# Hybrid attention layer on one core: the bank of weighted values is emptied by ScalarE, and GpSimd adds its pieces

## What is computed

```
...
def stick_breaking_attention(q, k, v):
...
        log_beta = jax.nn.log_sigmoid(z)
        log_stay = jnp.where(mask, jax.nn.log_sigmoid(-z), 0.0)
        later = lax.cumsum(log_stay, axis=3, reverse=True) - log_stay
        weights = jnp.where(mask, jnp.exp(log_beta + later), 0.0)
        return jnp.einsum('bhqk,bhkd->bhqd', weights.astype(v.dtype), v)
...
    o_sb = stick_breaking_attention(split_heads(q_sb, N_HEADS_SB), split_heads(k_sb, N_HEADS_SB),
                                    split_heads(v_sb, N_HEADS_SB))
    o_dl = dilated_mixture_attention(rotary(split_heads(q_dl, N_HEADS_DIL), positions),
                                     rotary(split_heads(k_dl, N_HEADS_DIL), positions),
                                     split_heads(v_dl, N_HEADS_DIL))
...
    return merged @ w_out
```

## Time and profile before

| | us |
|---|---|
| median of 3 runs | 2083.41 |
| lowest, highest | 2081.67, 2083.62 |
| profiled execution, its own time | 2083.61 |
| its span, first to last instruction | 2081.8 |
| TensorE busy | 1932.0 |
| VectorE busy | 1257.5 |
| ScalarE busy | 908.3 |
| GpSimd busy | 753.1 |

### The profile page before, as it was taken

The page is one execution under the profiler, slowest core; times in us unless marked ns, Lnnn a source line. Parts: engine busy times, 40 slices in busy tenths (PEclk is TensorE's granted clock), DMA queues, the critical chain, the costliest instruction groups (busy, mean ns, idle before and its releaser), DMA issues. The chain is left out here.

```text
span 2081.8 us, 25977 instructions
## 1 busy us (share of the span) xinstructions
PE 1932.0 (93%) x9224; PEld 1582.6 (76%) x9224; DVE 1257.5 (60%) x1649; ACT 908.3 (44%) x1467; POOL 753.1 (36%) x506
## 2 busy tenths in 40 slices
PE   5899999999999898989989976896999999999998
PEld 4788888888888676767767755685788888888886
DVE  6855556555556266676676677327856556554555
ACT  6433333333335455555555555306433333333334
POOL 2656656530000252242242335304656556540000
PEclk9999999999999999999999986897999999999999
DMA  3443544558664310010101112511534435458663
GB/s 143 153 166 131 193 151 144 190 192 290 195 192 144 116 46 26 21 56 25 51 25 40 31 36 70 193 41 71 186 143 160 174 132 185 152 203 308 192 192 142
DMA packets 95584, 276.01 MB, mean 133 GB/s; under 512 B 10480, under 2 KB 14704, under 8 KB 89840
## 3 DMA queue, kind: packets, MB, share of 16 engines
q1 hardware_dynamic: 95472, 274.59, 38.7%
HBM read 190.14 MB, written 80.22 MB: 130 GB/s over the span
## 5 line engine op out<-in xcount | busy, mean ns | idle before, releaser
L703 PE MATMUL banks<-ffn_x_operands_hi 128*128 128x512 f32 x616 | 239.8, 389 | 0.0
L706 PE MATMUL banks<-ffn_x_operands_hi,ffn_x_operands_lo 128*128 128x512 f32 x616 | 239.7, 389 | 0.0
L705 PE MATMUL banks<-ffn_x_operands_lo,ffn_x_operands_hi 128*128 128x512 f32 x616 | 239.6, 389 | 0.0
L1265 DVE TENSOR_TENSOR heads_wt<-banks,heads_wt 128x512 fp32r<-128x512 f32 (+1 forms) x160 | 100.9, 632 | 134.7 <-ACT heads_wt L1109 133.9
L1382 PE MATMUL banks<-first_hi,w_hi 128*128 128x512 f32 x384 | 161.1, 420 | 13.5 <-ACT heads_qk_raw L1131 7.9
L401 ACT ACTIVATE scaled_rows<-banks 128x512 f32<-128x512 f32 x132 | 78.6, 595 | 201.9 <-PE banks L690 201.9
L516 DVE TENSOR_TENSOR scaled_rows<-banks,scaled_rows 128x512 f32<-128x512 f32 x132 | 91.1, 690 | 118.1 <-PE banks L690 74.4
L986 POOL TENSOR_TENSOR scaled_rows<-scaled_rows,heads_stay 128x128 f32<-128x128 f32 (+7 forms) x64 | 86.1, 1351 | 210.9 <-DVE heads_stay L1225 210.9
L1384 PE MATMUL banks<-first_hi,w_lo 128*128 128x512 f32 x384 | 152.2, 396 | 0.0
L1383 PE MATMUL banks<-first_lo,w_hi 128*128 128x512 f32 x384 | 152.0, 396 | 0.0
L687 PE MATMUL banks<-first_hi,ffn_w_ring_hi 128*128 128x512 f32 x352 | 139.1, 395 | 11.8 <-DVE first_lo L567 11.8
(11 more groups left out here) (183 smaller groups left out, 4821.0 us busy)
## 6 DMA issues: line engine op xcount, KB each, us to landing
w_raw<-in_ffn_w_gate SPq DMA_DIRECT2D x22, 1024.0 KB, 6.8
ffn_up_raw<-in_ffn_w_up SPq DMA_DIRECT2D x22, 1024.0 KB, 6.1
ffn_down_raw<-in_ffn_w_down SPq DMA_DIRECT2D x22, 1024.0 KB, 4.9
down_operands<-ffn_down_raw SPq DMA_DIRECT2D x22, 1024.0 KB, 7.3
w_raw<-h_operands SPq DMA_DIRECT2D x52, 256.0 KB, 3.0
ffn_up_raw<-h_operands SPq DMA_DIRECT2D x52, 256.0 KB, 3.0
ffn_down_raw<-h_operands SPq DMA_DIRECT2D x50, 256.0 KB, 3.0
w_raw<-in_w_in SPq DMA_DIRECT2D x24, 512.0 KB, 4.0
```

The source lines that it names most:

```text
L703: pe.matmul(out, hi[:, 0, tok], hi[:, 1, :], start=(opens and c == 0), stop=False, skip_group_check=True)
L705: pe.matmul(out, hi[:, 0, tok], lo[:, 1, :], start=False, stop=False, skip_group_check=True)
L706: last = pe.matmul(out, lo[:, 0, tok], hi[:, 1, :], start=False, stop=(c == NP - 1), skip_group_check=True)
L1265: dve.tensor_tensor(wt[:, wt_slot(s, j), 0:tiles, 1, :], b.ps[:, bank, 0:tiles * P].rearrange("p (t c) -> p t c", c=P), wt[:, wt_slot(s, j ...
```

## The change

ScalarE now empties the whole bank with two copies: rows 0 to 63 (512 columns: both heads, high and low weights) to one of two new buffers `o_raw`, and the quarter low x high to one of two `o_low`, by even and odd steps. TensorE waits for the second copy (`o_low_done`) and no longer for `o_copied`. GpSimd makes both sums from SBUF, `o_low` += high x low, `o_stage` = high x high + `o_low`. Before it overwrites a pair of buffers, ScalarE waits until GpSimd is done with the step two back. In GpSimd's order the sums come at the end of a step, after products, rotation and weight splits; in the last run before that step's split of output weights. The first sums of GpSimd's loop are drawn out of it as on the other engines. To make room, the mask table, `o_low` and four small row buffers now share memory with others.

```diff
@@ build of buffers @@
-        mask_f = sb("mask_f", [P, 4, P])
...
-        o_low = sb("o_low", [HEAD, 2, P])
+        o_raw = [sb(f"o_raw{i}", [HEAD, 2, 2, P]) for i in range(2)]
...
-        stay = [[sb(f"stay{s}{a}", [P, SEQ + 1]) for a in range(2)] for s in range(2)]
+        stays = sb("stay", [P, 2, 2, SEQ + 1])
+        stay = [[stays[:, s, a, :] for a in range(2)] for s in range(2)]
+
+        o_low = [b.scaled[0:HEAD, 0:2, 0:P], stays[0:HEAD, 0, :, 0:P]]
+        mask_f = stays[:, 1, 1, 0:4 * P].rearrange("p (m c) -> p m c", c=P)
...
-        row_max, neg_max, row_sum, row_inv = (sb(n, [P, 4]) for n in ("row_max", "neg_max", "row_sum", "row_inv"))
+        row_max, neg_max = b.sumsq[:, 0:4], b.sumsq[:, 4:8]
+        row_sum, row_inv = b.root[:, 0:4], b.root[:, 4:8]
@@ gpsimd @@
+            def values_out(it, kind, s):
+
+                n = STEPS * run(it, kind) + s + 1
+                low, raw = o_low[s % 2], o_raw[s % 2]
+                if s % 4 == 0:
+                    pool.wait_ge(o_stored[s // 4], 32 * (run(it, kind) + 1))
+                pool.wait_ge(o_low_done, n)
+                pool.tensor_tensor(low, raw[:, :, 1, :], low, ALU.add).then_inc(o_low_sum, 1)
+                pool.wait_ge(o_low_sum, n)
+                pool.tensor_tensor(o_stage[:, :, s * P:(s + 1) * P], raw[:, :, 0, :], low, ALU.add
+                                   ).then_inc(o_copied, 1)
@@ gpsimd, end of step @@
                 if more_after(it, project) and ENDS.get(s) == 3:
                     split_weights(*pair_of(it, kind, 2), Q)
+                for j in range(banks_of(s)):
+                    if values_done(it, kind, s, j):
+                        values_out(*values_done(it, kind, s, j))
+                if last and s == STEPS - 1:
+                    values_out(it, kind, s)
...
+            one_run(0, SB_KIND, 0, 2)
             with pool.Fori(0, PAIRS - 1) as it:
-                one_run(it, SB_KIND)
+                one_run(it, SB_KIND, 2)
                 one_run(it, DIL_KIND)
-            one_run(PAIRS - 1, SB_KIND)
+                one_run(it + 1, SB_KIND, 0, 2)
+            one_run(PAIRS - 1, SB_KIND, 2)
@@ scalar @@
                 act.wait_ge(pv_ready, 4 + BANKS * run(it, kind) + bank_count(s + 1))
-                act.activation(o_low[:, :, :], values[HEAD:P, :, 0, :], ACT.Copy
-                               ).then_inc(o_low_done, 1)
+                if not (isinstance(it, int) and run(it, kind) == 0 and s < 2):
+                    act.wait_ge(o_copied, STEPS * run(it, kind) + s)
+                act.activation(o_raw[s % 2][:, :, :, :], values[0:HEAD, :, :, :], ACT.Copy)
+                act.activation(o_low[s % 2], values[HEAD:P, :, 0, :], ACT.Copy).then_inc(o_low_done, 1)
@@ vector @@
-            def values_out(it, kind, s):
...
-                dve.tensor_tensor(o_low[:, :, :], values[0:HEAD, :, 1, :], o_low[:, :, :], ALU.add
-                                  ).then_inc(o_low_sum, 1)
-                dve.wait_ge(o_low_sum, n)
-                dve.tensor_tensor(o_stage[:, :, s * P:(s + 1) * P], values[0:HEAD, :, 0, :], o_low[:, :, :], ALU.add
-                                  ).then_inc(o_copied, 1)
@@ tensor, weighted_values @@
                 if j == 0:
-                    pe.wait_ge(o_copied, 1 + STEPS * run(it, kind) + s)
+                    if not (isinstance(it, int) and run(it, kind) == 0 and s == 0):
+                        pe.wait_ge(o_low_done, STEPS * run(it, kind) + s)
```

More of the change, by code:

```diff
@@ L962, in _ @@
             sp.wait_ge(b.x_stored, 16 * TT)
-            for dst, src in ((mask_f[:, :, :], mask), (log_count_sb[:, :], log_count), (cos_sb[:, :], cos),
+            for dst, src in ((mask_f, mask), (log_count_sb[:, :], log_count), (cos_sb[:, :], cos),
                              (sin_sb[:, :], sin)):
@@ L1040, in split_out_weights, with one_run @@
                                    ).then_inc(out_w_split, 1)
-            def one_run(it, kind, project=True, last=False):
-                for s in range(STEPS):
+            def one_run(it, kind, first=0, end=STEPS, project=True, last=False):
+                for s in range(first, end):
                     step(it, kind, s, project, last)
@@ L1322, in step @@
                     weights_lo(it, kind, s, j, project)
-                    if values_done(it, kind, s, j):
-                        values_out(*values_done(it, kind, s, j))
                     if ahead and not leads and j == 0:
@@ L1335, in step @@
                     rotated_lo(*rot)
-                if last and s == STEPS - 1:
-                    values_out(it, kind, s)
             def one_run(it, kind, first=0, end=STEPS, project=True, last=False):
@@ L1350, in _ @@
             dve.wait_ge(tables_loaded, 16 * 4)
-            dve.tensor_copy(mask_r[:, :, :], mask_f[:, :, :])
+            dve.tensor_copy(mask_r[:, :, :], mask_f)
             for s in range(2):
```

## The result

Median of 4 runs 2102.67 us (2099.96 to 2103.51) against 2083.51 for 4 runs of the kernel before: ratio 1.0090, 95% interval 1.0076 to 1.0104. The kernel is 19 us **slower**; the forecast was 2083.9, the range ended at 2096.

The account below looks back on a forecast made before the run. TensorE, busy 93% of the span, was taken as the bound. Terms -11.8 - 3.2 + 2 + 8.4 + 2.3 + 2.6 = +0.3 us gave 2083.9 us, no difference; range 2071 to 2096.

Parts of the forecast that it names:

- the port: Heads stage: a VectorE instruction waits for one GpSimd instruction; GpSimd's sums mostly fit its idle time, 2 us on.
- the second rival: Stick-breaking steps 4 to 7: each of 16 steps loses one GpSimd sum, 0.73 us; 2093.6 us, chance 0.23.
- the clock: Heads stage: one in three new TensorE stops meets a stretch of lower granted clock, 2.3 us on.
- the tail: End of the heads stage: GpSimd's last sums delay the last weight split and the next block, 2.6 us on.
- The gain of the release and of VectorE's relief: Heads stage: sooner bank release takes 11.8 us off TensorE's waits, VectorE losing its sums another 3.2 us.
- the third rival: Waits at the bank are symptoms; half of the 15 us gain returns at the next wait; 2091.4 us, chance 0.08.
- the late swap: Dilated run ahead of a stick-breaking run, 3 times: swap transfers queue behind a store awaiting GpSimd's sum, 8.4 us on.
- the marks: Signs in the heads stage: bank waits under 20 us, three swap waits, projection-bank waits of 2.8 us, later next block.
- The mark against the forecast: Sign for the rival that the port decides: scans much longer than 2.9 us with GpSimd's sums beside them.

Follow-up runs that it names:

- e8: Against the changed kernel, GpSimd makes no sums, only waits for the low copy and counts; 2073.94 us, ratio to before 0.9949 to 0.9973.
- e9: Against the kernel before, VectorE's sums out of PSUM cover 8 of 128 columns, releasing the bank sooner without ScalarE's extra copy; 2070.95 us.

## Why the prediction was wrong

**The step that failed** is the port, in two places of the prediction. "A waiting VectorE instruction thus waits for one GpSimd instruction, not for the pair" was read from the earlier trace rows, where GpSimd's next product waited for that very scan. Sums that stand late in GpSimd's queue make the products ready, and then VectorE stood behind three instructions at 756.82 us. And the forecast's sum put GpSimd's 128 sums into its idle time, for +2 us. They cost 30.0 - 8.2 (the swap) = 21.8 us in the stage, or 1.4 us for each of the 16 large stick-breaking steps if it all fell there: about both sums, where the second rival had reckoned one (0.73 us, 11.7 in all). That rival had the mechanism and half the price. Put in full into the forecast's sum, 21.8 gives 2083.9 - 2 + 21.8 = 2103.7, against 2103.4 for the profiled execution. That agreement is luck: the 21.8 hold what the clock and the tail cost, which the sum has as terms of their own (4.9), and the gain fell short by 4.2, so two errors cancel.

A reading in the same paragraph was wrong too. The normalisation at 1261.17 does not read two wide tiles: it reads one, and a value per partition. It takes 2.18 us where the same shape just before took 0.55, and GpSimd's product ran beside it until 1263.00:

```profile
1260.51 0.55 DVE L1251 TENSOR_SCALAR scaled_rows<-scaled_rows,heads_row_inv 128x640 f32<-128x640 f32 x1
...
1261.11 1.89 POOL L1036 TENSOR_TENSOR w_raw<-w_raw,gains_sb 128x1024 f32<-128x1024 f32 x1 [0.79 <-ACT first_hi L1141]
```

So VectorE can stand with one wide tile from SBUF too. And it was done 0.35 us after that product. GpSimd's next instruction, at 1263.08, needed that product's result, while the products that passed the sine product needed nothing of the sum ahead of them. Whether this is what decides which engine is served next, no run shows.

**The gain of the release and of VectorE's relief:** -15.0 forecast, -10.8 measured with no sums at all (e8). By stretches, e8 gains 5.3 us in the three that are mostly dilated runs (the terms had 9 x 0.55 - 0.3 + 2.4 = 7.1), 2.5 in the last run (6 x 0.55 + 0.8 = 4.1) and 2.9 in the rest (7 x 0.55 = 3.9).

In the dilated runs the mechanism was the forecast one: of the 5.3 us, 4.5 are idle time that went. One of the three stretches, before and in e8:

```profile
812.16:906.05 93.89, 88.37 (x527) 69.93 (x526) 63.52 (x124) 51.14 (x103) 25.91 (x20) 1.00 0.16 46
```

```profile
811.74:903.15 91.41, 88.02 (x528) 69.98 (x527) 53.76 (x100) 57.55 (x117) 26.75 (x21) 1.00 0.17 47
```

In the last run it was another. The same matmuls, before and in e8:

```profile
1198.08:1308.52 110.44, 72.92 (x404) 59.68 (x403) 82.51 (x156) 59.30 (x107) 49.91 (x24) 0.76 0.22 65
```

```profile
1190.16:1298.10 107.94, 64.20 (x405) 51.83 (x403) 77.28 (x130) 64.67 (x120) 50.80 (x24) 0.86 0.22 68
```

TensorE is busy for 8.7 us less, at a mean granted clock of 0.86 in place of 0.76, and stands 6.2 us more: what came quicker was waited away for the most part. The waits at the bank shrank by 21 us over the stage (33.6 to 12.4), and others took their place, as the third rival has it. That TensorE's idle time in the whole stage is the same (83.4 and 83.6 us) is the sum of these opposite parts. In e9 the last run has 2.1 us less busy and 2.6 us less idle time, so the split between clock and waiting there differs from kernel to kernel.

**The clock** of the kernel after: +2.3 forecast, +5.7 us in busy time. No run tested by itself what decides which stretches run at the lower clock. A part looks like chance: both kernels stop for the same 2.08 us, ahead of 725.5 and 725.7 us, and only after the change the clock is at the lower level behind it (before, then after):

```profile
728.00:731.00 3.00, 3.00 (x19) 2.24 (x19) 1.55 (x4) 1.67 (x4) 0.15 (x1) 1.00 0.00 0
```

```profile
728.00:731.00 3.00, 3.00 (x10) 2.31 (x9) 0.48 (x1) 0.00 (x0) 0.00 (x0) 0.52 0.00 0
```

**Right:** the late swap, +8.4 forecast. TensorE falls back 3.0, 3.2 and 2.0 us at the three swaps, and putting the swap ahead of the store takes 8.2 off the stage (4.7 by the medians). The row of the wait:

```profile
898.14 0.69 DVE L1308 TENSOR_TENSOR heads_rot_swap<-heads_rot_swap,heads_sin 128x512 f32<-128x512 f32 x1 [3.20 <-DMA heads_rot_swap<-heads_qk_raw]
```

**The tail:** +2.6 forecast, 1.8 measured from the last low copy to the next block:

```profile
1315.40 0.38 ACT L1179 ACTIVATE heads_stay<-banks 64x256 f32<-64x256 f32 x1
...
1317.25 1.89 POOL L1057 TENSOR_TENSOR w_raw<-w_raw,gains_sb 128x1024 f32<-128x1024 f32 x1
1319.22 2.34 POOL L1060 TENSOR_TENSOR first_lo<-w_raw,first_hi 128x1024 fp32r<-128x1024 f32 x1
...
1321.88 0.95 SPq L1582 DMA_DIRECT2D scaled_rows<-o_between  x2
```

That is 1321.88 - 1315.78 = 6.1 us, against 1302.56 - 1298.27 = 4.3. ScalarE's copy of 64x512 was taken at 0.60 us and is 0.59.

**Of the marks** named ahead, bank waits under 20 us and three waits for the swap came. TensorE's waits for the projection bank at the swaps came too, but with 1.76, 1.94 and 1.72 us for 2.8, and the next block starts 4.6 us after the last sum, not 3 to 4. The mark against the forecast, scans much longer than 2.9 us with GpSimd's sums beside them, was a poor one: scans of 1024 columns rose from 2.61 to 3.19 us on the mean, but they take 3.19 in e8 as well, which has no sums. What the sums made long was the sine product.

The Trainium skill, page "SBUF — State Buffer", section "Who interferes with whom", gives the rule of the exclusive lock between the two engines, and says that a VectorE instruction with at most one SBUF input, outside its two-port modes, does not contend with GpSimd; a sum whose other operand lies in PSUM is such an instruction. With this rule the traces agree where it was tried: the sums out of PSUM beside the product (0.41 us), the same out of SBUF behind it (1.68 us), a sum of GpSimd behind a scan. It also says that the order of issue decides who blocks. That VectorE's instruction, begun at 756.82, was passed by two of GpSimd's, the first begun at 757.35, is more than it says.

## What to carry to other kernels

Before work is moved from PSUM to SBUF, count the instructions that need the shared port in the stretch that is on the path, in the order in which they take it: scan, product, scan, product is one queue for two engines. What an added instruction costs there is not its length but what it makes wait: full sums cost 21.8 us of the stage in the late place for 93 us of length, and tiny ones 8.5 for 28 (128 x 0.22). With an operand left in PSUM VectorE's sums slipped in beside GpSimd's product, 0.41 us each.

The waits of TensorE that a change attacks are not what it will gain. To price them, build a kernel that has the release and no new work: here it gained a third of the waits' sum. Then look at that gain by stretches, in idle and in busy time apart, since the total of each can hide two opposite parts.

## What the runs showed of the hardware

- A VectorE instruction that waits for the port can be passed by GpSimd instructions that are ready back to back: 3.67 us (behind one sum and two products), 4.57 and 4.74 us for one of 0.66.
- A VectorE instruction with one wide SBUF operand (L1251, a tile times a value per partition) can stand for GpSimd as well: 2.18 us beside a GpSimd product, 0.55 just before it.
- A GpSimd sum of 16 elements a partition takes 0.22 us free and 0.48 to 0.56 on the mean of its first place in the pair, up to 1.94 behind a scan; in the late place, 64 such pairs cost 8.5 us of the stage (6.6 by the medians).
- The last run's matmuls took 72.9 us at a mean granted clock of 0.76 and 64.2 at 0.86, and 6.2 of these 8.7 us came back as idle time.
